# An encoder layer on one core: value products in rounded passes, query squares split in two, the attention chain two steps later

## The reference

```python
mod = silu(c) @ w_ada + b_ada                       # six rows of shift, scale, gate
h = rms_norm(x, norm_mix_pre) * (1 + sc1) + sh1
aq, ak, av, hq, hf_f, hf_b, hi, hg = split(h @ w_in)
# attention group: 8 query heads of width 128, 2 key/value heads
q, k = rope(rms_norm(aq)) * 128 ** -0.5, rope(rms_norm(ak))
o_att = softmax(q @ k.T) @ v
o_hg = hgrn2(hq, hf_f, hf_b, hi, hg)                # 8 heads of a gated linear recurrence
x = x + g1 * rms_norm(concat(o_att, o_hg) @ w_out)
h = rms_norm(x, norm_ffn_pre) * (1 + sc2) + sh2
x = x + g2 * rms_norm(geglu(conv3(h @ w_up)) @ w_down)
```

## Time and profile before

| | us |
|---|---|
| median of 3 runs | 2370.38 (2370.3 to 2372.6) |
| the profiled execution | 2374.25 |
| its span, first to last instruction | 2372.5 |
| TensorE busy | 2330.9 (98% of the span) |
| VectorE busy | 1885.3 (79%) |
| ScalarE busy | 1108.4 (47%) |
| share of the last chain that is TensorE | 89% |

### The profile page before, as it was taken

One profiled execution on the slowest core, in us unless ns is written; L12 is line 12 of the kernel. 1 busy time (PEld: TensorE's weight loads), 2 busy tenths in 40 slices (PEclk: granted clock), 3 DMA queues, 4 the chain that ended last, 5 costly groups with the idle time before them and its releaser, 6 DMA issues.

```text
span 2372.5 us, 37255 instructions
## 1 busy us (share of the span) xinstructions
PE 2330.9 (98%) x13671; PEld 2027.8 (85%) x13671; DVE 1885.3 (79%) x2455; ACT 1108.4 (47%) x1524; POOL 128.6 (5%) x207
## 2 busy tenths in 40 slices
...
DMA packets 378834, 442.47 MB, mean 187 GB/s; under 512 B 14876, under 2 KB 295716, under 8 KB 376448
## 3 DMA queue, kind: packets, MB, share of 16 engines
...
...
## 4 chain that ended last, share of the span: by engine, by line
PE 89%; DVE 5%; DMA 2%; ACT 2%; issue 1%; SPq 0%; DVEq 0%; ACTq 0%
PE bank L2147 27%; PE bank L2149 27%; PE bank L2148 27%; DMA ADA<-in_w_ada_dram 2%; PE bank L2312 2%; DVE ACC L1383 1%; PE bank L2213 1%; PE bank L2331 1%; PE bank L2204 1%; DVE ZZ L1588 0%; PE bank L2398 0%; DVE W_lo L1342 0%; PE bank L2078 0%; PE bank L2500 0%; PE bank L2502 0%
## 5 line engine op out<-in xcount | busy, mean ns | idle before, releaser
L2147 PE MATMUL bank<-H_lo,W_hi 128*128 128x256 f32 (+1 forms) x1832 | 631.8, 345 | 1.1 <-DVE H_lo L1409 1.1
L2149 PE MATMUL bank<-H_hi,W_lo 128*128 128x256 f32 (+1 forms) x1832 | 612.0, 334 | 0.0
L2148 PE MATMUL bank<-H_hi,W_hi 128*128 128x256 f32 (+1 forms) x1832 | 611.7, 334 | 0.0
L2147 PEld LDWEIGHTS bank<-H_lo,W_hi 128*128 128x128 f32 x1832 | 348.5, 190 | 35.2 <-issue 4.6
L2149 PEld LDWEIGHTS bank<-H_hi,W_lo 128*128 128x128 f32 x1832 | 348.0, 190 | 35.1
L2148 PEld LDWEIGHTS bank<-H_hi,W_hi 128*128 128x128 f32 x1832 | 348.6, 190 | 33.8 <-issue 4.5
L2147 PE MATMUL bank<-T_lo,W_hi 128*128 128x256 f32 x1280 | 362.2, 283 | 0.0
L2148 PE MATMUL bank<-MGR,W_hi 128*128 128x256 f32 x1280 | 362.2, 283 | 0.0
L2149 PE MATMUL bank<-MGR,W_lo 128*128 128x256 f32 x1280 | 362.2, 283 | 0.0
L2147 PEld LDWEIGHTS bank<-T_lo,W_hi 128*128 128x128 f32 x1280 | 245.8, 192 | 0.0
L2148 PEld LDWEIGHTS bank<-MGR,W_hi 128*128 128x128 f32 x1280 | 245.8, 192 | 0.0
...
## 6 DMA issues: line engine op xcount, KB each, us to landing
AB_raw<-in_w_ada_dram SPq DMA_DIRECT2D x128, 512.0 KB, 4.4
...
```

Of the source, the lines that this page charges most:

```text
L2147: pe.matmul(acc, st_hi, mv_lo, start=start, stop=False, skip_group_check=on)
L2148: pe.matmul(acc, st_hi, mv_hi, start=False, stop=False, skip_group_check=on)
L2149: return pe.matmul(acc, st_lo, mv_hi, start=False, stop=stop, skip_group_check=on)
```

## The change

The value products of all heads go in three passes: ScalarE's copy of the turned probabilities is now rounded (PT_hi), VectorE subtracts it from the PSUM bank (PT_lo, `probs_low`, four times a head), and the values are split once for each run of heads with the same key/value head (heads 0, 3 and 7, `NEW_VALUES`), where VSA was copied for every head. The squares of the query are split too (SQA_hi on ScalarE, SQA_lo on VectorE, `squares_rest`), and the rotation sum is two passes. The attention chain moves by two steps: the rotation sum from step 1 to 2, the scores from step 7 to 9, the transposes from step 12 to 14, the value products from step 4 of the next head to step 7. VectorE's rotation is cut in two (`rope_back` in step 2, `rope_scale` in step 6). The chunk rows of the first recurrence head and the two splits of a tile have other steps. In ScalarE's, VectorE's and TensorE's lists `att_tail` now stands ahead of `att_side` or has more in it. SP's and GpSimd's lists are unchanged.

```diff
-    VSA = at("VSA", [P, TT, P], F32, OV + 8 * KB)
...
+    SQA_hi, SQA_lo = at("SQA_hi", [P, S], F32R, OV + 8 * KB), at("SQA_lo", [P, S], F32R, OV + 12 * KB)
+    QT = at("QT", [P, S], F32, OV + 38 * KB)
+    PM = [at(f"PM{n}", [P, S], F32, OV + (18 + 2 * n) * KB) for n in range(TT)]
+    PT_lo = at("PT_lo", [P, TT, TT, P], F32R, OV + 18 * KB)
+    PT_hi = at("PT_hi", [P, TT, S], F32R, OV + 26 * KB)
+    V_hi, V_lo = at("V_hi", [P, TT, P], F32R, OV), at("V_lo", [P, TT, P], F32R, OV + 2 * KB)
...
-        CHUNK_STEPS_0 = (7, 14, 17, 17, 23, 30, 33, 33, 39, 46, 49, 49, 55, 62, 66, 70)
+        CHUNK_STEPS_0 = (3, 5, 7, 9, 19, 21, 23, 25, 35, 37, 39, 41, 51, 53, 66, 70)
...
+        LATE = 2
+        NEW_VALUES = [h for h, n in enumerate(HEADS) if h == 0 or n // 4 != HEADS[h - 1] // 4]
...
                 act.activation(SQA[:, :], src, ACT.Square).then_inc(rope_in, 1)
+                if r >= KV_HEADS:
+                    act.wait_ge(rope_in, 2 * r - KV_HEADS + 1)
+                    act.activation(SQA_hi[:, :], SQA[:, :], ACT.Copy).then_inc(rope_in, 1)
...
+                if qt == 0 and h:
+                    act.wait_ge(att_pv, h)
...
-                act.activation(PT[:, :, qt * P:(qt + 1) * P],
+                act.activation(PT_hi[:, :, qt * P:(qt + 1) * P],
...
+            def values_hi(h):
...
+                act.activation(V_hi[:, :, :].rearrange("p a b -> p (a b)"), V2[:, HEADS[h] // 4, :], ACT.Copy).then_inc(v_hi, 1)
...
             def att_side(h, s):
                 if s == 0:
                     query_front(h)
-                if s == 2:
+                if s == 3:
                     rope_rs(h + KV_HEADS)
-                if s == 5:
+                if s == 5 + LATE:
                     queries_hi(h)
-                if 8 <= s < 12:
-                    att_exp(h, s - 8)
-                if s == 12:
-                    vsa_copy(h)
-                if s >= 13:
-                    pt_copy(h, s - 13)
+                if 0 <= s - 8 - LATE < TT:
+                    att_exp(h, s - 8 - LATE)
+                if s == 14 and h in NEW_VALUES:
+                    values_hi(h)
+                if s >= 13 + LATE:
+                    pt_copy(h, s - 13 - LATE)
 
             def att_tail(h, s):
-                if s == 1:
-                    pt_copy(h, TT - 1)
-                if s == 5:
+                if s < 1 + LATE:
+                    pt_copy(h, s + TT - 1 - LATE)
+                if s == 6 + LATE:
                     att_store(h)
...
+                    if k >= 2:
+                        att_tail(k - 2, s)
...
-                    if g % 8 == 3:
-                        split_hi(i, 20, U_HG + 10 * e + LEAD + g // 8)
+                    if g % 16 in ((3, 7) if first and e == 0 else (3, 11)):
+                        split_hi(i, 20, U_HG + 10 * e + LEAD + g // 8 + (1 if first and e == 0 and g % 16 == 7 else 0))
...
-                for kt in gates:
-                    chunk_row(0, kt)
+
+            def rope_scale(r, dst):
...
+            def squares_rest(n):
+                dve.wait_ge(rope_in, KV_HEADS + 2 * n + 2)
+                dve.tensor_tensor(SQA_lo[:, :], SQA[:, :], SQA_hi[:, :].bitcast(F32), ALU.subtract).then_inc(squares_low, 1)
...
+            def values_low(h):
+                dve.wait_ge(v_hi, NEW_VALUES.index(h) + 1)
+                dve.tensor_tensor(V_lo[:, :, :].rearrange("p a b -> p (a b)"), V2[:, HEADS[h] // 4, :],
+                                  V_hi[:, :, :].rearrange("p a b -> p (a b)").bitcast(F32), ALU.subtract).then_inc(kv_lo, 1)
+
+            def probs_low(h, qt):
+                dve.wait_ge(pt_ready, h * TT + qt + 1)
+                dve.tensor_tensor(PT_lo[:, qt, :, :], PB[6 + qt % 2][:, :].rearrange("p (k q) -> p k q", q=P),
+                                  PT_hi[:, :, qt * P:(qt + 1) * P].bitcast(F32), ALU.subtract).then_inc(pt_low, 1)
...
-            def att_side(h, s, gates=()):
+            def att_side(h, s):
                 if s == 1:
-                    rope_query(h, gates)
+                    squares_rest(h)
+                if s == 2:
+                    rope_query(h)
                 if s == 6:
+                    rope_scale(h + KV_HEADS, QT[:, :])
+                if s == 6 + LATE:
                     queries_low(h)
-                if 8 <= s < 12:
-                    att_max(h, s - 8)
-                if 9 <= s < 13:
-                    att_scale(h, s - 9)
+                if 0 <= s - 8 - LATE < TT:
+                    att_max(h, s - 8 - LATE)
+                if 0 <= s - 9 - LATE < TT:
+                    att_scale(h, s - 9 - LATE)
+                if s >= 13 + LATE:
+                    probs_low(h, s - 13 - LATE)
+                    if h in NEW_VALUES:
+                        values_low(h)
+
+            def att_tail(h, s):
+                if s < 1 + LATE:
+                    probs_low(h, s + TT - 1 - LATE)
...
-                    if g % 8 == 4:
+                    if first and e == 0:
+                        if g % 16 in (4, 8):
+                            split_lo(i, 20, U_HG + 10 * e + LEAD + g // 8)
+                    elif g % 8 == 4:
                         split_lo(i, 20, U_HG + 10 * e + LEAD + g // 8)
                     if first and e == 0:
-                        if g in CHUNK_STEPS_0 and g % 16 != 1:
+                        if g in CHUNK_STEPS_0:
...
-                pe.wait_ge(rope_in, r + 1)
+                if r < KV_HEADS:
+                    pe.wait_ge(rope_in, r + 1)
+                else:
+                    pe.wait_ge(rope_in, 2 * r - KV_HEADS + 2)
+                    pe.wait_ge(squares_low, squares_low_base + r - KV_HEADS + 1)
                 if r == 0:
                     pe.wait_ge(front_kept, 1)
                 else:
                     pe.wait_ge(rope_ln, r)
                 if r >= KV_HEADS + 2:
                     pe.wait_ge(att_out, r - KV_HEADS - 1)
-                pe.matmul(PB[2][:, :], ones[:, :], SQA[:, :], start=True, stop=True).then_inc(rope_psum, 1)
+                if r < KV_HEADS:
+                    pe.matmul(PB[2][:, :], ones[:, :], SQA[:, :], start=True, stop=True).then_inc(rope_psum, 1)
+                else:
+                    pe.matmul(PB[2][:, :], ones_r[:, :], SQA_hi[:, :], start=True, stop=False)
+                    pe.matmul(PB[2][:, :], ones_r[:, :], SQA_lo[:, :], start=False, stop=True).then_inc(rope_psum, 1)
...
-                    pe.wait_ge(pt_ready, n - 1)
+                    pe.wait_ge(pt_low, pt_low_base + n - 1)
...
-                pe.wait_ge(vsa_ready, h + 1)
+                pe.wait_ge(pt_low, pt_low_base + h * TT + TT)
+                pe.wait_ge(kv_lo, 1 + sum(1 for n in NEW_VALUES if n <= h))
+                acc = PB[2][:, :].rearrange("p (t q) -> p t q", q=P)
                 for k in range(TT):
-                    ins = pe.matmul(PB[2][:, :], VSA[:, k, :], PT[:, k, :], start=(k == 0), stop=(k == TT - 1))
+                    pe.matmul(acc, V_hi[:, k, :], PT_lo[:, :, k, :], start=(k == 0), stop=False)
+                    pe.matmul(PB[2][:, :], V_hi[:, k, :], PT_hi[:, k, :], start=False, stop=False)
+                    ins = pe.matmul(PB[2][:, :], V_lo[:, k, :], PT_hi[:, k, :], start=False, stop=(k == TT - 1))
                 ins.then_inc(att_pv, 1)
 
             def att_side(h, s):
-                if s == 1:
+                if s == 2:
                     rope_mm(h + KV_HEADS)
-                if 7 <= s < 11:
-                    scores(h, s - 7)
-                if s >= 12:
-                    turn_probs(h, s - 12)
+                if 0 <= s - 7 - LATE < TT:
+                    scores(h, s - 7 - LATE)
+                if s >= 12 + LATE:
+                    turn_probs(h, s - 12 - LATE)
 
             def att_tail(h, s):
 
-                if s == 4:
+                if s < LATE:
+                    turn_probs(h, s + TT - LATE)
+                if s == 5 + LATE:
                     att_values(h)
```

More of the change, by code:

```diff
@@ L221, in hybrid_encoder_layer @@
     T1 = at("T1", [P, S], F32, OV + 16 * KB)
-    QT = at("QT", [P, S], F32, OV + 20 * KB)
-    PM = [at(f"PM{n}", [P, S], F32, OV + o * KB) for n, o in enumerate((22, 24, 18, 38))]
-    PT = at("PT", [P, TT, S], F32, OV + 26 * KB)
+    SQA_hi, SQA_lo = at("SQA_hi", [P, S], F32R, OV + 8 * KB), at("SQA_lo", [P, S], F32R, OV + 12 * KB)
[4 more added lines that the diff above has]
+    V_hi, V_lo = at("V_hi", [P, TT, P], F32R, OV), at("V_lo", [P, TT, P], F32R, OV + 2 * KB)
     COS = at("COS", [P, S], F32, OV + 34 * KB)
@@ L327, in hybrid_encoder_layer @@
         v_copied, v_turned, v_ready = sem("v_copied"), sem("v_turned"), sem("v_ready")
-        vsa_ready = sem("vsa_ready")
-        k_hi, k_lo, q_hi, q_lo = sem("k_hi"), sem("k_lo"), sem("q_hi"), sem("q_lo")
+        v_hi = sem("v_hi")
+        pt_low, pt_low_base = vec_ready, 1
+        squares_low, squares_low_base = c_ready, 1
+        k_hi, kv_lo, q_hi, q_lo = sem("k_hi"), sem("kv_lo"), sem("q_hi"), sem("q_lo")
```

(24 more changed lines are left out.)

6 lines of the change are left out of this document (2 added, 4 removed).

## The result

The changed kernel takes 2398.03 us (median of 4 runs, 2397.71 to 2401.25) against 2371.49 before on the same chip (2370.3 to 2375.09): a ratio of 1.0117, 95% interval 1.0105 to 1.0129. It is slower by 26.5 us. The forecast was 2388, the range 2374 to 2400.

The account below looks back on a forecast made before the run. TensorE, busy 98% of the span, was taken as the bound. Heads' stretch +17.8, scores 0 later by 2.2, less 1.37 and 0.7, gave +17.9: 2392 for the profiled execution, 2388 on the median, range 2374 to 2400.

Parts of the forecast that it names:

- The saving: TensorE, value products and rotation sum: fewer passes save 0.705 and 0.41 us a head, 8.9 us over eight heads.
- Waits one and two: TensorE waits for SQA_lo at the rotation sum, 1.5 us; Q_lo puts scores 7.96 us after that sum in heads 0-3.
- Wait three: Heads 4 to 7: chunk rows ahead of Q_lo, the third awaiting AB_raw under 4 to 6; scores start late.
- The landing that I took: AB_raw load for the third chunk row under heads 4 to 6: taken to land in 4.8 us.
- the clock rival: Waits of 4.7 to 6.2 us lower TensorE's clock, 1.5 to 4 us each time: 2392 to 2402, chance 0.27.
- Small waits: AB_raw loads land in time, only waits one and two remain: 2378, 2372 to 2382, chance 0.15.
- The gain arrives: Q_lo ends before TensorE comes to the scores, SQA_lo below 2.8 us into the period: 2357, chance 0.12.
- Losses and gains about equal: Whole kernel: the losses cancel the gains, 2366 to 2375, chance 0.04.
- Capacity, the rival of the experiments: VectorE has more work than TensorE has time under heads 4 to 6, so reordering only moves waits; no chance given.

Follow-up runs that it names:

- row_at_16: Kernel after with query scaling, Q_hi, Q_lo early in all heads, SQA_lo ahead of the third PT_lo, chunk rows spread, one in the next head's step 0: 2365.52 us.
- squares_first: Kernel after with SQA_lo ahead of the third PT_lo in VectorE's list, nothing else: 2394.77 us, ratio 1.0107 to before.
- before_rows: Kernel before with only its chunk rows moved early, the third between the W_lo of step 4 and Q_lo: 2403.58 us, ratio 1.0130.
- old_rows: Kernel after with only the steps of the chunk rows put back as before the change: 2378.39 us, ratio 1.0036 to before.
- warm: Kernel after with 18, 26, 26 and 8 idle TensorE passes ahead of the first score product of heads 4, 5, 6 and 7: 2392.05 us.
- row_at_18: Like row_at_16, but with that chunk row in step 2 of the next head instead of step 0: 2368.58 us, ratio 0.9987 to before.

## Why the prediction was right in kind and 10 us short

**The saving is real.** Twelve value passes take 188.92 to 191.64, 2.72. Where nothing waits (row_at_16, heads 1 to 4) a period is 18.60 us; 18.65 was predicted.

**Waits one and two hold.** The rotation sum waited 1.2 us under heads 1 to 4 (predicted 1.5) and 0.8 under 5 to 7 (1.0). But the sum's wait is not what these heads hang on alone: squares_first took it away and won back 0.3 of the 1.2 us a head, since Q_lo was only just in time. From the sum to the first score product heads 1 to 3 took 8.06 (7.96); head 0, counted from the start of K_lo, came 2.4 later than before (2.2).

**Wait three holds.** From the rotation sum to the scores: head 4 12.73 us (12.7), heads 5 and 6 14.5 and 14.7 (14.2), head 7 10.46 (10.3). TensorE waited 4.53, 6.32, 6.49 and 2.26 (4.7, 6.2, 6.2 and 2.3). before_rows and old_rows show that the place of the chunk rows carries the loss: +31.6 us from it in the kernel before, and 19.6 less without it in the kernel after. The landing that I took (4.8) fits head 5: the load went out at 280.13 and its chunk row started at 285.01, 4.9 later.
From the fit of the Trainium skill (DMA: Bandwidth & Descriptors, "Anatomy of one DMA"), which the page gives for DMAs that GpSimd issues in software while SP issues these, the prediction had an estimate of 4.0 us for a load behind another. Under heads 4 to 6 the trace has 4.6 at the least and 5.3 in the median from issue to landing; the measurement decides.

**What failed is the choice between the forecast and the clock rival.** I let the waits cost their own length. That the clock falls behind them had 0.27, with 1.5 to 4 us each; it fell behind all four. Against the predicted periods that is 2.9, 2.4 and 1.7 us, and 1.5 behind head 7. The argument against, head 0's wait of 2.02 us that left the clock alone, was read from a wait less than half as long as the three that mattered. Warm measures it from the other side: 6.0 us less in the median. So the range was right, and held the measured time because it had been drawn to take in part of this rival; the likeliest value was not.
By the sentence of the Trainium skill cited with that rival (TensorE: Matmul & The Clock Gate, "What's actually happening"), activity is what releases the throttle. Warm's passes, which compute nothing that is used, agree: 1.00 where the kernel after has 0.50.

**How the 10 us add up.** The profiles start the heads at different times, which goes mostly with the clock of an earlier stretch: from 94 to 110 us the granted clock is 0.68 before, 0.89 after, and anything up to 1.00 in the others, and K_lo starts at 166.3, 162.5 and as early as 162.2. (At one clock, 0.79, before_rows has it at 165.2 and three edits of the kernel after at 163.8 to 164.2, so about 1 us of this may be the kernel's.) So I compare from the start of K_lo to the end of the span: 2206.25 before, 2233.38 after, +27.1, close to the medians' +26.5. Predicted was +17.9. The 9.2 between them are 7.5 in the seven periods, 1.5 behind head 7 and 0.2 at head 0. Most of it is clock: the part of the granted clock that is missing in the two-us windows from each of the four resumptions on comes to 2.6, 1.9, 1.5 and 1.7 us, an estimate of 7.7. The subtraction alone would not show it behind head 7, since from its first score product to the end of the span kernels with the clock at 1.00 there take from 2053.8 us (warm) to 2058.5 (row_at_18), and after 2057.1. The median of before, 1.1 higher in this comparison, is the rest.

**The other rivals.** Small waits (2378) fell with the AB_raw waits of 3.3 to 3.7 us. The gain arrives (2357) fell at its own test: SQA_lo was not there by 2.8 us into the period. With the lists put in a better order it does arrive in part, at 2365.5. Losses and gains about equal fell with the 26.5 us.

**Capacity, the rival of the experiments,** is not needed for the loss: before_rows has it without VectorE's new work, and row_at_16 is faster than before with all of it. It may be part of what is left: in row_at_16 VectorE is busy 36.4 and 35.5 of 40 us from 240 and from 280 us on, and the three periods from head 4 on are 1.3 to 2.1 us over 18.6. How much of that is VectorE's and how much the other work of those steps, no run separates; before has 0.7 on top there as well.
